# Two transformer layers and a second block at 256 tokens: layer seams laid anew, two gate rows sent through memory

## What is computed

```python
def _layer(x, ...):                       # twice
    h = _rms_norm(x, g_pre)
    proj = h @ w_in                       # queries, keys, values, gates of three attentions
    ...
    y = concatenate([o_a, o_b, o_c]) @ w_out
    return x + _rms_norm(y, g_post)

def second_block(x, c, ...):
    mod = silu(c) @ w_ada + b_ada
    shift1, scale1, gate1, shift2, scale2, gate2 = ...      # six rows of D
    h = rmsnorm(x, g_norm_mix) * (1.0 + scale1) + shift1
    ...                                   # sparse attention and retention on h @ w_in
    x = x + gate1 * (concatenate([o_nsa, o_ret]) @ w_out)
    h2 = rmsnorm(x, g_norm_ffn) * (1.0 + scale2) + shift2
    x = x + gate2 * peer_ffn(h2, w_q, sub_keys, u, v)
    return rmsnorm(x, g_norm_final)
```

## Time and profile before

| | |
|---|---|
| median of 3 runs | 2913.14 us (2911.41 to 2915.44) |
| profiled execution | 2914.45 us |
| its span | 2912.8 us |
| TensorE busy | 2877.8 us (99%) |
| VectorE busy | 2123.5 us (73%) |
| ScalarE busy | 1316.2 us (45%) |
| GpSimd busy | 399.9 us (14%) |
| DMA | 620.59 MB, mean 213 GB/s |

### The profile page before, as it was taken

How to read it: one execution, slowest core, us unless ns; L and a number is a source line. 1 busy time by engine, 2 the same in 40 slices (tenths; PEclk the granted TensorE clock), 3 DMA queues, 4 the chain that set the end, 5 groups by cost and what they waited for, 6 DMA issues and landing times.

```text
span 2912.8 us, 42860 instructions
## 1 busy us (share of the span) xinstructions
PE 2877.8 (99%) x15946; PEld 2472.4 (85%) x15946; DVE 2123.5 (73%) x2854; ACT 1316.2 (45%) x1677; POOL 399.9 (14%) x390
## 2 busy tenths in 40 slices
PE   9999999999999999999999999999999999999998
PEld 7888788888888888988888888888888888887886
DVE  6697776687776857877588787448874488888745
ACT  5443544443543334755355444444444444444433
POOL 1134010133021101020088200000000000000001
PEclk9999999999999999999999999999999999999999
DMA  9867477866568867266455444555445454445543
GB/s 344 306 214 274 177 255 276 303 228 248 194 224 287 302 251 257 80 245 224 168 188 188 187 182 178 189 197 185 179 175 200 187 188 178 174 181 180 193 190 144
DMA packets 100413, 620.59 MB, mean 213 GB/s; under 512 B 11088, under 2 KB 11216, under 8 KB 38096
## 3 DMA queue, kind: packets, MB, share of 16 engines
q1 hardware_dynamic: 71360, 509.88, 47.0%
q0 software_dynamic: 28944, 109.26, 10.6%
HBM read 616.99 MB, written 2.10 MB: 213 GB/s over the span
## 4 chain that ended last, share of the span: by engine, by line
PE 85%; DVE 5%; DMA 5%; ACT 2%; issue 1%; POOL 1%; SPq 0%; POOLq 0%; DVEq 0%; ACTq 0%
PE ps L586 27%; PE ps L1057 17%; PE ps L596 14%; PE ps L540 14%; PE ps L1133 6%; DMA aring<-in_ada 5%; DVE wl L2001 2%; PE ps L1015 1%; DVE aring L2017 1%; ACT BIG L1223 1%; ACT wh L1223 1%; PE ps L778 1%; PE ps L818 0%; PE ps L894 0%; PE ps L698 0%
## 5 line engine op out<-in xcount | busy, mean ns | idle before, releaser
L1223 ACT ACTIVATE wh<-ring 128x2048 fp32r<-128x2048 f32 (+2 forms) x499 | 895.0, 1800 | 1272.7 <-PE ps L596 645.9
L2001 DVE TENSOR_TENSOR wl<-ring,wh 128x2048 fp32r<-128x2048 f32 (+1 forms) x433 | 990.0, 2287 | 482.4 <-ACT stage_h L1223 249.7
L586 PE MATMUL ps<-hhl,wh 128*128 128x512 f32 x3680 | 884.6, 392 | 0.2 <-ACT wh L1223 0.2
L586 PEld LDWEIGHTS ps<-hhl,wh 128*128 128x128 f32 x3680 | 677.1, 189 | 132.5 <-issue 0.9
L596 PEld LDWEIGHTS ps<-hhl,wl 128*128 128x128 f32 x3680 | 471.6, 191 | 19.6 <-DVE wl L2001 1.9
L596 PE MATMUL ps<-hhl,wl 128*128 128x256 f32 x3680 | 477.5, 283 | 0.7 <-DVE wl L2001 0.6
L540 PE MATMUL ps<-wh,hhl 128*128 128x512 f32 (+1 forms) x1728 | 404.1, 386 | 2.5 <-issue 2.3
L540 PEld LDWEIGHTS ps<-wh,hhl 128*128 128x128 f32 x1728 | 319.1, 188 | 65.3 <-issue 3.3
L2017 DVE SCALAR_TENSOR_TENSOR aring<-aring,BIG 128x1024 f32<-128x1024 f32 x192 | 233.9, 1221 | 85.7 <-DMA aring<-in_ada 84.7
L540 PE MATMUL ps<-wl,hhl 128*128 128x512 f32 (+1 forms) x864 | 209.3, 384 | 2.4 <-DVE wl L2001 2.4
L1057 PE MATMUL ps<-wh,stage_h 128*128 128x512 f32 x736 | 196.9, 389 | 0.0
(11 more groups left out here) (327 smaller groups left out, 2585.6 us busy)
## 6 DMA issues: line engine op xcount, KB each, us to landing
...
```

Source lines behind the costliest of these rows:

```text
L586: mm(ps[:, 4 + c, :], wh[:, c % 2, k * P:(k + 1) * P], hhl[:, k, :, :].rearrange("p a b -> p (a b)"), start=(k == 0), stop=False, skip_gro ...
L1223: return nc.scalar.activation(o, i, func, **kw)
L2001: return tt(blocks(wl[:, c % 2, :], cols), blocks(ring[:, c, :], cols), blocks(wh[:, c % 2, :].bitcast(F32), cols), ALU.subtract)
```

## The change

Five things:

- **First products** of each layer on half a quarter (`first_slice`): four matmuls with `hh` of the first two banks' first part as soon as it is there, four with `hl`, the next transposes, the other half, then the eight with `wl`. In layer 0 ACT makes the first half of `wh` one bank earlier; `keep_awake` 8 to 5.
- **Last unit of WO and WO2**: tile 0's twelve matmuls first, `tile_full` behind them; ACT's square, DVE's `Y` and `shares` of tile 0 follow it while tile 1's twelve run. `wl` of this unit is needed after 8 matmuls, not 16. DVE's `next_low` for the stage behind moves behind the modulation tile (WO) or behind X (WO2). `keep_awake` 20 to 15 and 12 to 8.
- **Mean steps** fused from four two-column steps to four one-column ones with nothing between them.
- **Seam to the second block**: transposes of part 0, nine `keep_awake`, gates of part 0, then transposes of part 1; DVE's list is laid anew.
- **Gate rows**: one matmul turns both gates into 32 partitions by 128, ACT copies them to `spare`, waiting for it ahead of `wh` of unit (1,0); POOL stores them to memory (`gate_rows`, 16 KB) ahead of tile 4, and behind tile 5 it waits for the store and loads `grow` (1 MB, one row to all partitions); `gate2row` likewise behind the keys. ACT no longer copies rows. The norm of X's last block moves from ACT to POOL (L1907 after). DVE takes two modulation tiles at j = 12 and none at j = 14.

The diff, cut:

```diff
-                    if n == 16:
+                    if n == (8 if by_tile else 16):
                         split(g, s)
-                    t, kk, j = (n // 8, n // 2 % 4, n % 2) if n < 16 else (n // 4 % 2, n % 4, 2)
+                    if by_tile:
+                        t, kk, j = (n // 12, n % 12 // 2, n % 2) if n % 12 < 8 else (n // 12, n % 12 - 8, 2)
+                    elif by_pair and n < 16:
+                        t, kk, j = n // 2 % 2, 2 * (n // 8) + n % 2, n // 4 % 2
+                    else:
+                        t, kk, j = (n // 8, n // 2 % 4, n % 2) if n < 16 else (n // 4 % 2, n % 4, 2)
                     tok, w, k = slice(t * P, (t + 1) * P), slice(kk * 512, kk * 512 + cols), 4 * place[s] + kk
                     lhs, rhs = ((hh, wh), (hl, wh), (hh, wl))[j]
                     last = mm(ps[:, 2 * pair + t, 0:cols], lhs[:, k, tok], rhs[:, s % 2, w], start=s == 0 and kk == 0 and j == 0,
                               stop=s == R - 1 and kk == 3 and j == 2, skip_group_check=True)
                 return last
+
+            def first_slice(g, pair, cols, place, l):
+
+                for half in range(2):
+                    pe.wait_ge(nh_done, l * 8 + half + 1)
+                    if l == 0 and half == 0:
+                        pe.wait_ge(hi_first, 1)
+                    else:
+                        pe.wait_ge(hi_done, g * R + 1)
+                    rows_slice(g, 0, pair, cols, place, 8 * half, 8 * half + 4, by_pair=True)
+                    pe.wait_ge(nl_done, l * 8 + half + 1)
+                    settle()
+                    rows_slice(g, 0, pair, cols, place, 8 * half + 4, 8 * half + 8, by_pair=True)
+                    if half == 0:
+                        transposed(l, 1)
+                rows_slice(g, 0, pair, cols, place, 16, 24).then_inc(unit_done, 1)
 
             def rows_group(g, n, pair, cols=512, use=None, layer=None, after_first=None, place=(0, 1, 2, 3), begun=False, rest=None, between=None, tile=None):
...
-                    rows_group(gw + i, l * TM_N + (TM_G + i), i % 2, use=None if i else l, place=PLACE, begun=i == 0)
-                keep_awake(20, 7)
-            keep_awake(12, 7)
+                    rows_group(gw + i, l * TM_N + (TM_G + i), i % 2, use=None if i else l, place=PLACE, begun=i == 0,
+                               tile=tile_full if i == WO_G - 1 else None)
...
             transposed(LAYERS, 0, TM2_BANKS, Xn)
-            transposed(LAYERS, 1, TM2_BANKS, Xn)
+            keep_awake(9, 7)
             pe.wait_ge(c2_ready, 16)
             gates(0)
+            transposed(LAYERS, 1, TM2_BANKS, Xn)
...
-                    gate_row(GATE_MIX, (4, 5, 6, 7)).then_inc(g1_full, 1)
-            pe.wait_ge(grow_done, 1)
-            pe.wait_ge(tm_free, N_WO2 + WO_G + 1)
-            gate_row(GATE_FFN, (0, 1, 6, 7)).then_inc(g2_full, 1)
-            keep_awake(6, 4)
+                    mm(ps[0:2 * KD, 4, 0:P], mod[:, GATE_MIX * KD:(GATE_FFN + 1) * KD], ident, start=True, stop=True).then_inc(gates_turned, 1)
+            pe.wait_ge(gates_copied, 1)
+            keep_awake(20, 5)
             prenorm(LAYERS + 1, WQ_BANKS)
 
...
                 act.wait_ge(gg_done, 8 * l + 6)
-                act.wait_ge(unit_done, g * R + R)
                 for t in range(T):
                     if t:
-                        act.wait_ge(yg_done, 5 * l + 4)
+                        act.wait_ge(unit_done, g * R + R)
+                    else:
+                        act.wait_ge(tile_full, l + 1)
                     f(lsquares[:, t, 0:512], ps[:, 2 + t, :], ACT.Square, scale=DM ** -0.5,
...
                         next_high(G_WO2 + i, c)
-                    if i == 1 and c == 0:
-                        act.wait_ge(g1_full, 1)
-                        act.wait_ge(hl_done, (LAYERS + 2) * 4)
-                        f(grow.rearrange("p (a b) -> p a b", a=4), ps[:, 4:8, :], ACT.Copy).then_inc(grow_done, 1)
+                    if i == 0 and c == 2:
+                        act.wait_ge(gates_turned, 1)
+                        f(spare[0:2 * KD, 0:P], ps[0:2 * KD, 4, 0:P], ACT.Copy).then_inc(gates_copied, 1)
                     if i and c >= R - T:
                         t = c - (R - T)
...
-            next_high(G_WQ, 0)
             for t in range(T):
                 act.wait_ge(x_done, T * (LAYERS + 1) + t + 1)
                 f(Xn[:, t, (WO_G - 1) * 512:DM], X[:, t, (WO_G - 1) * 512:DM], ACT.Square, scale=DM ** -0.5,
                   accum_out=ypart[:, t, WO_G - 1:WO_G]).then_inc(sq_done, 1)
-
-            act.wait_ge(g2_full, 1)
-            act.wait_ge(a_used, ADA_UNITS + 2)
-            for half, bank in ((0, 0), (1, 6)):
-                f(gate2row[:, half * (DM // 2):(half + 1) * (DM // 2)], ps[:, bank:bank + 2, :], ACT.Copy).then_inc(g2_done, 1)
-            act.wait_ge(prs_done, LAYERS + 2)
-            act.sem_inc(act_passed, 1)
-            for t in range(T):
-                f(Xn[:, t, 3 * 512:DM], X[:, t, 3 * 512:DM], ACT.Copy, scale=rstd2[:, t:t + 1]).then_inc(xn_last, 1)
+            next_high(G_WQ, 0)
+
             act.wait_ge(gsc_done, 2)
...
                 rsqrt([(sums, sums, HD)], sums, rw[:, 8 * i:8 * i + 8], rrs_done)
-            modulation(A_WO2 // 2, ADA_WO2)
+            for n in range(4):
+                tile(A_WO2 + n)
+            pool.wait_ge(gates_copied, 1)
+            pool.dma_start(gate_rows.rearrange("j (k p) -> (j k) p", p=P), spare[0:2 * KD, 0:P]).then_inc(rows_stored, 16)
+            for n in range(4, 6):
+                tile(A_WO2 + n)
+            pool.wait_ge(rows_stored, 16)
+            pool.wait_ge(hl_done, (LAYERS + 2) * 4)
+            pool.dma_start(grow, gate_rows[0:1, :].to_broadcast([P, DM])).then_inc(grow_done, 16)
+            modulation(A_WO2 // 2 + 3, ADA_WO2 - 6)
...
+                pl.tensor_scalar(Xn[:, t, 3 * 512:DM], X[:, t, 3 * 512:DM], rstd2[:, t:t + 1], None, ALU.mult).then_inc(xn_last, 1)
             pool.wait_ge(a_used, ADA_UNITS + 2)
             pool.dma_start(keyT.rearrange("p a b -> p (a b)"), keys).then_inc(keys_ready, 16)
+            pool.dma_start(gate2row, gate_rows[1:2, :].to_broadcast([P, DM])).then_inc(g2_done, 16)
             u0 = G_OF["U0"] * R
             for j in range(1, PART):
                 c = j % R
...
+                    x_block(LAYERS - 1, 2)
+                    shifted(1)
+                    next_block(LAYERS - 1, 2)
+                    low_part(parts[1], use, 1)
+                    x_block(LAYERS - 1, 3)
+                    next_block(LAYERS - 1, 3)
+                    next_low(weights, 0)
+                    shifted(2)
+                    next_low(weights, 1)
+                    shifted(3)
+                    low_part(parts[2], use, 2)
+                    low_part(parts[3], use, 3)
                 dve.wait_ge(hl_done, use * 4 + 4)
                 dve.sem_inc(dve_passed, 1)
 
...
 
-            def mean_steps(l):
-
-                st(tt(part_a, gsum3, yr, ALU.mult))
-                x_piece(l, 1, 0)
+            def mean_steps():
+
+                for t in range(T):
...
                             shares(t, i - 1)
                 w = columns(WO_G - 1)
-                dve.wait_ge(unit_done, (g0 + WO_G) * R)
-                tt(Y[:, 1, w], ps[:, 3, :], gpost[:, w], ALU.mult).then_inc(yg_done, 1)
-                dve.wait_ge(ylast_sq, l + 1)
-                tt(Y[:, 0, w], ps[:, 2, :], gpost[:, w], ALU.mult).then_inc(yg_done, 1)
-                for t in (1, 0):
-                    dve.wait_ge(yg_done, 5 * l + (4 if t else 5))
+                next_low(g0 + WO_G - 1, R - 1)
+                for t in range(T):
+                    if t:
+                        dve.wait_ge(tm_free, l * TM_N + (TM_N + 2))
+                    else:
+                        dve.wait_ge(ylast_sq, l + 1)
+                    tt(Y[:, t, w], ps[:, 2 + t, :], gpost[:, w], ALU.mult).then_inc(yg_done, 1)
+                    dve.wait_ge(yg_done, 5 * l + 4 + t)
                     shares(t, WO_G - 1)
 
...
                 else:
-                    st(tt(part_a, gsum3, yr, ALU.mult))
-                    x_piece(l, 0, 0)
-                    st.done()
-                    st(tt(part_b, part_a, xsum3, ALU.add))
-                    x_piece(l, 0, 1)
-                    st.done()
-                    st(tt(part_c, part_b, yr, ALU.mult))
-                    x_piece(l, 1, 0)
-                    st.done()
-                    st(tt(xmean, part_c, xmean, ALU.add))
+                    mean_steps()
                     st.done()
                     ts(ms2, xmean, 0.0, EPS, ALU.max, ALU.add).then_inc(mean_done, 1)
-                    x_piece(l, 1, 1)
+                    x_block(l, 0)
 
...
             for j in range(WO_G * R):
-                if j > 1:
+                if 1 < j < WO_G * R - 1:
                     next_low(G_WO2 + j // R, j % R)
                 i, c = j // R, j % R
-                for _ in range(0 if j == WO_G * R - 1 else 2 if j in (2, 3, 6, 7, 10) else 1):
```

(4 more changed lines are left out.)

105 lines of the change are left out of this document (54 added, 51 removed).

## The result

| | before | after |
|---|---|---|
| median of 20 runs | 2913.16 us (2910.38 to 2917.26) | 2919.66 us (2916.02 to 2930.09) |
| span of the profiled execution | 2912.8 us | 2919.4 us |

The change makes the kernel slower by 6.5 us: the ratio is 1.0024, with an interval from 1.0018 to 1.0031. The forecast was 2913.8, its range 2906.0 to 2920.5; the median lies inside it, 0.84 us from its end, and on the side to which I gave 0.19.

A forecast was written before the change was run, and what follows sets the result against it. TensorE, busy 99% of the span at the upper clock, was taken to bound the kernel. The terms 0 - 1.75 - 1.1 + 3.5 + 0 gave +0.65 us, so a median of 2913.8 us, range 2906.0 to 2920.5.

The forecast's parts named there:

- The start: First products: they may start 0.7 us earlier, but a later wait takes it back; 0 us.
- Layer 0 to 1: Seam between the layers: POOL starts 0.67 us earlier and the first unit needs fewer operands; -1.75 us.
- Seam to the second block: Seam before the second block: one square less behind the unit and fused mean steps; -1.1 us, bounds 0.6 to 2.3 gained.
- The sum of the seams: The two seam terms together, from layer 0 to 1 and to the second block: -2.85 us.
- WO2: WO2 stage: the 1 MB load makes modulation tiles late, delaying unit (3,0) by 3.0 and the end by 0.5 more; +3.5 us.
- WO2 to WQ: Behind WO2: X ends earlier, but POOL's steps are held by wl and its norm is hidden; 0 us.
- The tile loop falls behind: Rival in WO2: tile 6 lands after 1290, the lag stays and TensorE waits; +7.65 us, 2920.8; chance 0.2.
- The seams give nothing: Rival at the seams: earlier starts only wait for the next tile or wl; +3.5 alone stands, 2916.6; chance 0.1.

The follow-up runs named there:

- e5: The kernel before with 12 of the 16 matmuls of the first gate row left out; median 2912.35 us, ratio 0.9999.
- e1: The changed kernel with the WO2 stage and all behind it as before, only start and layer seams new; median 2910.35 us, ratio 0.9990.
- e13: The whole change with the last modulation tiles at the places of before and the norm of X's last block on ACT; median 2913.74 us, ratio 0.9998.
- e2: The changed kernel with WO2's last unit, its modulation tiles, the next wl and ACT's squares in the old order; median 2914.32 us, ratio 1.0007.
- e7: e2 with the norm of X's last block on ACT instead of POOL; median 2911.88 us, ratio 0.9990.
- e3: The changed kernel with both gate rows and the norm made as before, WO2's last unit as changed; median 2918.23 us, ratio 1.0020.
- e8: e3 with the modulation tiles at the places of before; median 2911.16 us, ratio 0.9987.
- e9: e3 with 12 dummy products between matmuls 8 and 9 of the last unit of WO2; median 2914.91 us, ratio 1.0000.

## Why the prediction came out as it did

That the median lies in the range is owed to the range's width and in part to luck: the sum had +0.65 us, measured were +6.5, and the traces have two larger errors against each other, 5.07 us won by G where I had 2.85 (some 2 of them by chance, as e5 shows), and 10.15 lost behind it where I had 3.5.

- **The start, 0.** Right: the first product came 1.1 us sooner and the one behind the wait at 39 us 0.06 later, for the reason given.
- **Layer 0 to 1, -1.75.** Right: 8.42 to 6.32 us, -2.1. POOL's power starts 1.34 us after the unit's end (423.28 - 421.94), before 2.39 (424.16 - 421.77), as one square lies under it; I had 0.67 of that 1.05; the rest is mostly POOL's small step ahead of the power, 0.19 us instead of 0.52.
- **Seam to the second block, -1.1.** Half right: the transposes came 1.34 us sooner, the first unit 0.51, just under the lower bound of 0.6. The 0.67 at the front was not there. POOL's first power did start 1.07 us sooner after the unit's end, but DVE's mean steps start 3.73 us after it, before 3.63, since DVE's last sum ends 3.2 us after it, before 2.9. The second power comes 4.85 us after the unit's end instead of 6.37, 1.5 sooner and not 2.5, all of it by the fused steps. The blocks of X ahead of `low_part`, which I had named against it, took more.
- **The sum of the seams, -2.85,** stands against e1's -3.4, whose interval reaches from 0 to 5.5.
- **WO2, +3.5.** This is the step that failed. In the profiles G to E grew by 10.15 us. Its first half, a lag of 4.5 us that reaches (3,0) as 3.0, went by the right places: tile 6 came at 1282.94, which is 1288.0 on the clock of before (forecast 1287.5), and `wl` of (3,0) is used 4.4 us later after G than before. In the other traces with this load in POOL's list that is 1.4 (e13), 1.7 (e2) and 5.7 us (e7), so 3.0 lies among the sizes that occur; how much of the lag the bytes made and how much the order of the lists stays open. Its second half, "0.5 more, as j = 12 takes a tile more and the loop is then nearly done", is the error: from (3,0) to E the change takes 23.85 us, before 18.13, so 5.7 us more and not 0.5. I had seen that the tile loop was at its limit and yet counted an earlier tile as only DVE's 1.2 us of work. It is a wait for a transfer: tiles 18 and 19 can't be used earlier than they land, and everything behind them on DVE's list (the block of Y and X, `wl` of (3,3)) moves with the wait. e3 against e8 shows 7.1 us for it by the medians, 5.7 by the two traces (G to E 76.52 and 70.80).
- **A second effect that I had not costed:** behind that wait TensorE ran 12 matmuls at half clock, 1.7 us in the change. e9 takes it away. I had read the upper clock "throughout" from slices of 73 us; in stretches of 2 us the trace of before has it down to 0.50 at 1072 us and to 0.54 at 1248.
- **WO2 to WQ, 0.** The profiles give 0.8 us in sum, within the bounds. That POOL's small step would be held by the moved `wl` was right (1.32 us instead of 0.19), and the power ends 4.7 us after the last unit (forecast 4.8). The norm on POOL was mis-sized: at most 1.29 us each and hidden, I said; it was 1.76 us each, and it slowed DVE's norm, for which TensorE waits. The pairs under e7 give 1.3 to 1.5 us for it, near the upper bound of 1.5 that I had kept for a second hold.
- **The rivals.** "The tile loop falls behind" came nearest: slower, with waits at (1,2), (2,1), (3,0) and in the last unit. Its cause was another, though: on the clock of before tile 6 was used at 1288.0, short of the 1290 from which I let it decide, and e13, with the same rows from memory, has no wait in the last unit. "The seams give nothing" is refuted by S, 5.16 us earlier, and by e1, though by its time only just.
